# Loading the expert weights of a mixture of experts from two DMA queues in place of one

## The reference, cut to what matters

```python
N_EXPERTS, TOP_K, D_FF = 32, 4, 1024
logits = h @ router_w + router_b
top_v, top_i = lax.top_k(logits, TOP_K)
gates = jax.nn.softmax(top_v, axis=-1)
...                                        # tokens sorted by expert
def expert_block(args):
    xb, e = args
    hid = xb @ w1[e] + b1[e]               # w1[e]: 1024 x 2048
    return clamped_swiglu(hid[:, :D_FF], hid[:, D_FF:]) @ w2[e] + b2[e]   # w2[e]: 1024 x 1024
```

## Time and profile before

| | |
|---|---|
| median of 3 runs | 1848.69 us (1848.0 to 1850.47) |
| the profiled execution, its own time | 1848.19 us |
| its span, first to last instruction | 1846.4 us |
| mean granted TensorE clock | 0.953 |
| TensorE matmul busy | 1689.1 us (91%) |
| ScalarE busy | 278.6 us (15%) |
| DMA | 546.97 MB, mean 296 GB/s |
| the one queue that SyncE feeds (q1) | 529.82 MB, 70.8% of 16 engines' span |
| experts: first ranked block issued, last block landed | 286.0 us, 1197.0 us |

### The profile page before, as it was taken

How to read it: one execution, slowest core, us unless ns; L and a number is a source line. 1 busy time by engine, 2 the same in 40 slices (tenths; PEclk the granted TensorE clock), 3 DMA queues, 4 the chain that set the end, 5 groups by cost and what they waited for, 6 DMA issues and landing times.

```text
span 1846.4 us, 19987 instructions
## 1 busy us (share of the span) xinstructions
PE 1689.1 (91%) x8316; PEld 1033.2 (56%) x8316; DVE 473.0 (26%) x1015; ACT 278.6 (15%) x572; POOL 131.7 (7%) x265
## 2 busy tenths in 40 slices
PE   6999999967898599957899996899999999999997
PEld 3644684423344144413344442387777888888886
DVE  4545512101112012201111220245566312111101
ACT  3114421101011011101011110023214300200000
POOL 5781000000000000000000000010003000000000
PEclk7999999978999799978999998999999999999998
DMA  9566386999999999999999999963443344525340
GB/s 377 190 233 217 134 365 276 404 419 426 426 426 426 428 426 422 426 427 427 421 427 427 426 426 427 418 225 129 139 160 114 114 142 177 205 92 181 127 170 24
DMA packets 93918, 546.97 MB, mean 296 GB/s; under 512 B 6539, under 2 KB 18455, under 8 KB 62844
## 3 DMA queue, kind: packets, MB, share of 16 engines
q1 hardware_dynamic: 88960, 529.82, 70.8%
q0 software_dynamic: 4128, 14.42, 2.2%
q10 hardware_dynamic: 732, 1.38, 0.2%
HBM read 540.33 MB, written 7.62 MB: 297 GB/s over the span
## 4 chain that ended last, share of the span: by engine, by line
PE 64%; DMA 20%; SPq 1%; issue 0%; DVE 0%; ACT 0%; DVEq 0%
PE PS L1388 16%; DMA ring<-in_w 10%; DMA arena<-in_w 9%; PE PS L2338 8%; PE PS L1413 8%; PE PS L2177 5%; PE PS L2364 4%; PE PS L2190 3%; PE PS L2198 3%; PE PS L1364 2%; PE PS L2184 2%; PE PS L1424 2%; PE PS L2328 2%; PE PS L2206 1%; PE PS L1398 1%; PE PS L2224 1%
## 5 line engine op out<-in xcount | busy, mean ns | idle before, releaser
L1388 PE MATMUL PS<-arena 128*64 128x512 f32 (+2 forms) x984 | 273.0, 652 | 58.2 <-DMA ring<-in_w 40.2
L1388 PE MATMUL PS<-ring,arena 128*64 128x512 f32 (+2 forms) x928 | 224.6, 648 | 41.5 <-DMA arena<-in_w 28.2
L1388 PEld LDWEIGHTS PS<-arena 128*64 128x64 f32 (+2 forms) x984 | 84.2, 139 | 198.8 <-issue 198.2
L1388 PEld LDWEIGHTS PS<-ring,arena 128*64 128x64 f32 (+2 forms) x928 | 68.0, 136 | 154.5 <-issue 154.0
L2338 PE MATMUL PS<-arena,ring 128*128 128x256 f32 x704 | 152.6, 379 | 0.0
L1413 PE MATMUL PS<-ring,arena 128*64 128x512 f32 (+2 forms) x576 | 139.7, 615 | 12.4 <-DMA ring<-in_w 7.8
L1660 DVE TENSOR_SCALAR arena<-PS 128x512 f32<-128x512 f32 x28 | 19.4, 692 | 502.7 <-PE PS L1398 502.7
L2338 PEld LDWEIGHTS PS<-arena,ring 128*128 128x128 f32 x704 | 133.5, 190 | 18.0
L1413 PE MATMUL PS<-arena 128*32 128x512 f32 (+2 forms) x392 | 97.0, 630 | 9.7 <-DMA arena<-in_w 5.1
L1413 PEld LDWEIGHTS PS<-ring,arena 128*64 128x64 f32 (+2 forms) x576 | 45.9, 135 | 86.2 <-issue 86.2
L2177 PE MATMUL PS<-arena,ring 128*128 128x256 f32 x384 | 84.8, 380 | 0.0
(11 more groups left out here) (470 smaller groups left out, 2068.6 us busy)
## 6 DMA issues: line engine op xcount, KB each, us to landing
ring<-in_w SPq DMA_DIRECT2D x92, 2048.0 KB, 21.8
arena<-in_w SPq DMA_DIRECT2D x74, 2048.0 KB, 23.1
ring<-in_w_ada SPq DMA_DIRECT2D x24, 1024.0 KB, 9.6
arena<-in_w SPq DMA_DIRECT2D x24, 1024.0 KB, 20.4
cst<-in_w SPq DMA_DIRECT2D x24, 1024.0 KB, 21.0
ring<-in_w_in SPq DMA_DIRECT2D x22, 1024.0 KB, 12.1
ring<-in_w_up SPq DMA_DIRECT2D x20, 1024.0 KB, 7.7
ring<-in_w_gate SPq DMA_DIRECT2D x16, 1024.0 KB, 6.4
```

Source lines behind the costliest of these rows:

```text
L1388: m = pe.matmul(bank(("up", i, b))[rows[n], :], xs[:, k, rows[n]], tiles[n][:, b * 512:(b + 1) * 512], start=k == 0, stop=False, skip_grou ...
```

## The change

Of the blocks from number 49 on, those with an even place in the list (50, 52, ..., 254: 103 blocks) are now issued by ScalarE on its own queue. SyncE issues 49, 51, ..., 255 and, behind them as before, the blocks of the following layer. ScalarE's loads are woven into its steps: ahead of step s it issues all of its blocks, in order, whose `after` lies at or below `behind[s]`, the number of TensorE steps planned before step s. Sources, places and the value of `after` of every block are what they were, and so are the instructions of TensorE, VectorE and GpSimd.

```diff
--- before.py
+++ after.py
@@ -1,3 +1,4 @@
+import itertools
 from contextlib import ExitStack
 
 import concourse.bass as bass
@@ -94,6 +95,7 @@
         self.slots, self.turn, self.fills, self.spent_at = list(slots), 0, {}, {}
         self.added_at = {}
         self.loads, self.weights, self.open, self.homes, self.held = [], {}, {}, [], []
+        self.behind = {}
 
     def rotate(self, banks):
         self.banks, self.at = list(banks), -1
@@ -1227,6 +1229,7 @@
         def plan_experts(x, p, steps):
             p.rotate(range(4, 8))
             for s in steps:
+                p.behind[s] = p.n
                 kind = s[0]
                 i = s[1] if len(s) > 1 else 0
                 r0, lanes, first, width = x.units[i]
@@ -1300,6 +1303,7 @@
         MAIN_STEPS = list(expert_steps(0, len(MAIN_UNITS), SORT))
         plan_experts(EXPERTS, plan, MAIN_STEPS)
         MAIN_N, MAIN_USES, MAIN_LOADS = plan.n, list(plan.uses), len(plan.loads)
+        FIRST_RANKED = min(i for i, one in enumerate(plan.loads) if one.rank is not None)
         dve_own_more = sem("dve_own_more")
         more = Plan([])
         more.homes = WHOLE[:7] + [(NS, NS + NX + N1)]
@@ -1496,8 +1500,13 @@
                 o = g_of[key].bank * 512
                 return PS[:, o + a:o + b]
 
+            mine = plan.loads[FIRST_RANKED + 1:MAIN_LOADS:2] if x.first else []
+            known = {}
             for s in steps:
                 kind = s[0]
+                ready = list(itertools.takewhile(lambda one: one.after <= x.plan.behind[s], mine))
+                mine = mine[len(ready):]
+                load_all(act, w, ready, pe_done, slot_in, known)
                 if kind == "gather":
                     i = s[1]
                     for c in range(2):
@@ -1752,24 +1761,24 @@
                     dve.tensor_copy(gS, bank(("permute",), 64, 128).rearrange("p (a b) -> p a b", a=2)).then_inc(moved[g.bank], 1)
                     w.wait_ge(moved[g.bank], g.use)
 
-        def load_all(sp, w, loads, done, filled):
-            known = {}
+        def load_all(queue, w, loads, done, filled, known=None):
+            known = {} if known is None else known
             for one in loads:
                 if one.slots is None:
                     v = slot_view(one.slot)[:, 0:one.m * one.n].rearrange("p (k n) -> p k n", k=one.m)
                     w.wait_ge(row_added, one.added)
                     w.wait_ge(done, one.after)
-                    sp.dma_start(v, one.src.rearrange("(k p) n -> p k n", p=128)).then_inc(filled[one.slot], 16)
+                    queue.dma_start(v, one.src.rearrange("(k p) n -> p k n", p=128)).then_inc(filled[one.slot], 16)
                     continue
                 src, a = one.src, (one.part or 0) * SLOT
                 if one.rank is not None:
                     if one.rank not in known:
                         w.wait_ge(ids_ready, 1)
-                        known[one.rank] = sp.value_load(ids[0:1, one.rank:one.rank + 1], min_val=0, max_val=NE - 1)
+                        known[one.rank] = queue.value_load(ids[0:1, one.rank:one.rank + 1], min_val=0, max_val=NE - 1)
                     src = src[bass.ds(known[one.rank], 1), :, :]
                 w.wait_ge(done, one.after)
                 rows = src.rearrange("e (p j) n -> p e (j n)", p=128)[:, :, a:a + one.m * SLOT]
-                sp.dma_start(slot_view(one.slot, one.m).unsqueeze(1), rows).then_inc(filled[one.slot], 16)
+                queue.dma_start(slot_view(one.slot, one.m).unsqueeze(1), rows).then_inc(filled[one.slot], 16)
 
         def all_done(w, x):
 
@@ -2923,7 +2932,8 @@
             sp.dma_start(xv, I["xT"].rearrange("(k p) t -> p k t", p=128)).then_inc(x_in, 16)
             load_all(sp, w, plan.loads[:10], pe_done, slot_in)
             sp.dma_start(ctxT, I["ctxT"].rearrange("(k p) t -> p k t", p=128)).then_inc(ctx_in, 16)
-            load_all(sp, w, plan.loads[10:MAIN_LOADS], pe_done, slot_in)
+            load_all(sp, w, plan.loads[10:FIRST_RANKED], pe_done, slot_in)
+            load_all(sp, w, plan.loads[FIRST_RANKED:MAIN_LOADS:2], pe_done, slot_in)
             w.wait_ge(most_ready, 1)
             with sp.If(sp.value_load(most[0:1, 0:1], min_val=0, max_val=512) > S):
                 inside = Waits(sp)
```

## The result

The changed kernel takes 1865.29 us (median of 4 runs, 1862.94 to 1866.23), the kernel before beside it 1849.15 (1848.0 to 1850.47): a ratio of 1.0086, 95% interval 1.0073 to 1.0099, or some 16 us slower. The forecast was 1856: the direction held, and 7.5 us of the 16 were forecast. The profiled execution after took 1865.55 us, with a span of 1863.7.

A forecast was written before the change was run, and what follows sets the result against it. The prediction took DMA transfer in the experts as the bound. Issuing 0, rate 0 and lateness 4 + 2.4 + 1.9 = 8.3, taken as 7.5 us, gave 1856 us as a median, range 1846 to 1867.

The forecast's parts named there:

- place 1: `down` of unit 2: ScalarE's blocks stand behind the copy, DMA dry 4 us (5.3 worked out, bounds 0 and 5.3).
- place 2: Units 4 and 5: TensorE lags 8.5 us for ScalarE's late blocks, DMA dry 2.4 us (bounds 0 and 10.9).
- place 3: `down` of unit 8, same pattern as in unit 2: DMA dry for 1.9 us (bounds 0 and 5).
- Part 1, issuing itself: Issues moved from SyncE to ScalarE: 0, never the bound; five blocks of unit 4 cost ScalarE about 3.5 us.
- Part 2, the rate: DMA rate in the experts with two queues: 0, bounds +5% and -5%, 45 us of some 910 us of transfer.
- Part 3, lateness: ScalarE issues late, behind its copies: the DMA goes dry at three places, sum 8.3 us, 7.5 taken.
- Elsewhere: 0: Other places in the experts: ScalarE's blocks wait some microseconds at most, covered by blocks in flight; 0, uncovered 1 to 3 us.
- Larger lag: Rival: ScalarE's blocks come at half the engines, units 4 and 5 cost 10.9 us, units 7 and 10 2 to 4 each; 1866, chance 0.12.
- A rising rate: Rival: two queues hide what one leaves between packets, so blocks come sooner; 1845 us at +1.2%, chance 0.14.
- No change: Rival: 4 to 9 us in hand and SyncE's earlier issue cover all places; 1849 to 1851 us, chance 0.16.
- the likeliest case: The forecast itself, slower through late issues by ScalarE: 1851 to 1862 us, chance 0.58.

The follow-up runs named there:

- e2: Against the kernel before: SyncE alone issues on one queue, even blocks held back until the steps ScalarE would have waited for; 1853.29 us, ratio 1.0028.
- e1: Against the changed kernel: ScalarE issues blocks freed midway in `down` or by the last slice of `up` ahead of its copy or sigmoids; 1863.61 us, ratio 1.0078.
- e9: Against the changed kernel: every expert block split by columns, halves on SyncE's and ScalarE's queues, in the order of before, ahead of ScalarE's waits; 1863.55 us, ratio 1.0089.
- e12: Against the changed kernel: SyncE alone issues both column halves of every expert block, one behind the other, on its one queue; 1863.89 us, ratio 1.0088.
- e3: Against the changed kernel: GpSimd issues the even blocks on its software queue as soon as a place is free; 1863.29 us, ratio 1.0073.
- e4: Against the changed kernel: ScalarE's 2 MB blocks go as two transfers with 8 KB rows in place of one with 16 KB rows; 1886.09 us, ratio 1.0204.
- e10: Against the changed kernel: SyncE alone issues every expert block as two transfers of 64 partitions on its one queue; 2623.12 us, ratio 1.4235.
- e5: Against the changed kernel: every expert block split by partitions, 0 to 63 on SyncE's queue, 64 to 127 on ScalarE's, in one order, issued early; 2433.18 us.

## Why the prediction was half right

| term | forecast, us without data | after | one queue, late (`e2`) | early (`e1`) |
|---|---|---|---|---|
| place 1, 509 to 525 us | 4 | 4.9 | 5.3 | 3.0 |
| place 2, about 600 us | 2.4 | 0.4 | 0 | 2.2 |
| place 3, 925 to 955 us | 1.9 | 5.1 | 3.8 | 3.5 |
| unit 3, 488 to 507 us | none | 5.5 | 0 | 5.6 |
| 720 to 727 us | none | 2.5 | 0 | 4.1 |
| 811 to 817 us | none | 4.2 | 0 | 0 |

(Each number is counted from the rows' records as above, for `e2` at place 3 with 0.5 us from 921 us on; each run has small ones besides.)

*Part 1, issuing itself: 0.* Right, as far as the runs show. ScalarE's five issues behind the copy at 519.32 us took until 523.0, 3.0 us from the first on against 3.5 taken, and TensorE waited for the copies of `gather` 0.5 us in all of the experts. `e9` and `e12` issue two transfers for each block, on two engines and on one, and are within 0.3 us of each other.
*Part 2, the rate: 0.* Right, and the bounds of 5% were far too wide: 426 to 428 GB/s in full slices. The rule of the Trainium skill that the prediction cited ("DMA: Bandwidth & Descriptors", "Issuing engines are not separate DMA queues") agrees with the trace. But the term was read as if a rate were all that sharing changes. That is the step that failed.
*Part 3, lateness.* The mechanism is real: 8.3 us without data forecast, 9.1 counted in `e2` at places 1 and 3, worth 5 us of time in that run. That the two sums are close is luck in part. Place 1 is right (4 taken, 5.3 worked out, 5.3 counted in `e2`); place 2 fell out, and place 3 was twice what I took. In the changed kernel lateness explains less: of place 1 `e1` keeps 3.0 of 4.9 us without it.
*Place 2* was worked out with a lag for TensorE and none for the DMA. TensorE does lag: the place of block 117 is filled from 600.7 us in place of 585.4, 15.3 later. But the blocks in flight lag too, by what went dry before: block 116 lands at 604.4 in place of 594.3, and 0.4 us are lost.
*Place 3* has the same pattern as unit 3, since unit 9 has one lane, and a lateness that I had put at 0. Of its 5.1 us only 0.9 lie behind 941 us, where the copy of `down` holds back block 192 and the ones behind it:

```profile
946.74 0.60 ACT L1540 ACTIVATE arena<-PS 128x512 f32<-128x512 f32 x1 [17.48 <-PE PS L1417]
947.42 0.34 ACTq L1781 DMA_DIRECT2D ring<-in_w  x1
```

Ahead of that block 190 stands behind a sigmoid (L1534). TensorE is done with its place at 925.3 us (the end of its 20.60 us below), ScalarE issues it at 928.78, it lands in 9.0 us, and `down` waits for it. From the chain that ended last:

```profile
904.70 20.60 PE PS L1392 x48
...
928.63 0.06 ACT arena L1534
...
928.78 9.02 DMA ring<-in_w
...
937.94 8.78 PE PS L1417 x64
```

*"Elsewhere: 0."* Wrong, and the bulk of the miss. I priced blocks that land at half the rate only for the group behind place 1. From block 50 on it holds in every group. It also put the waits behind sigmoids at 0, which block 190 shows to be too little where no backlog covers them. The sharing is worth 14 us alone (`e1`, `e3`), lateness 5 alone (`e2`), both 16. They don't add up; place 2 shows one reason, a delay of TensorE that the DMA has by then as well.
*The rivals.* "Larger lag" named 1866, which is the time, but by luck. Its sum doesn't give it: 1848.7 + 7.5 + 8.5 are 1865 already, and 2 to 4 more at each of two units make 1869 to 1873. And it has another mechanism: it put 10.9 us at place 2, where 0.4 are lost. It had the right thought, ScalarE's blocks at half the engines, at the wrong place. A rising rate is excluded by the full slices at 425 to 428. "No change" fell by the dips.
*The range* of 1846 to 1867 held the time; the likeliest case's own, 1851 to 1862, did not. What the forecast rests on is worth 5 us by itself. That the wide range held is owed to the order of the blocks, which it had no term for, and so to luck.
Not followed: the last block lands 20.4 us later, and the span is only 17.3 longer. Some 1.6 us are made good between the landing and the last `scatter` and 1.4 behind it. Nor was it isolated why the dip at 811 us is in the changed kernel and not in `e1`.

## What to carry to other kernels

Where one queue already fills the DMA engines, its order is the schedule. A second queue adds no rate and takes the order away: whatever is queued on it gets every other row, needed or not. Before splitting a stream by turns, look at what stands in the other queue when the most urgent block is in flight; if a split is wanted, put parts of the same block on both, over all 128 partitions, and with rows as long as before if they can be (this last was not tested). And a control that changes two things (two queues and short rows) needs its own control.

## What was not expected of the hardware

- Turns between two queues go by rows, of 8 KB as of 16 KB: 53 against 54 rows in 3 us, 0.44 against 0.88 MB. Halving the rows of one of them cost 21 us (`e4`), of which some 9 can be plain rate.
- Transfers to 64 partitions, 0 to 63 or 64 to 127, move 215 GB/s on one queue and 240 with both halves at once on two, against 427 for 128 partitions, with the engines shown as full. A 16 KB row took 1210 ns in `e10`, 993 in `e5`, 618 before (means over 900 to 1000 us). The Trainium skill ("SBUF — State Buffer", section "Door 1: The DMA port swizzle") says that bandwidth depends on how many of 16 ports the partitions reach, and by its map partitions 0 to 63 reach 8, and 64 to 127 the other 8. 215 GB/s, half of 427, agrees.
- Rows of 8 and 4 KB in place of 16 and 8 cost 1.7% of the rate, on one queue as on two: a row of 8 KB takes 314.6 ns in `e9`, half of one of 16 KB is 309.
